# The projection of p moved from the keys stage into the last block of each tile, and the output formed and stored in halves

## The reference

```
h = h + (sum_b sigmoid(gate_b) * (branch_b @ W_b)) @ W_out
h = h + PEER(RMSNorm(h))                               # sum over 128 experts per token of w * v_row
h = h + sigmoid(RMSNorm(h) @ W_g) * (p[i] @ W_p)       # p: (1024, 256), W_p: (256, 1024)
```

## Time and profile before

| what | us |
|---|---|
| median of three runs | 3938.55 |
| the profiled execution's own time | 3932.46 |
| its span | 3930.7 |
| keys stage | 0 to 239 |
| branches stage | 240 to about 765 |
| late stage, before rows are fetched | to about 976 |
| rows being fetched and used | to 3898 |
| last block of tile 7 | 3898 to 3930.7 |

### The profile page before, as it was taken

The page is one execution under the profiler, slowest core; times in us unless marked ns, Lnnn a source line. Parts: engine busy times, 40 slices in busy tenths (PEclk is TensorE's granted clock), DMA queues, the critical chain, the costliest instruction groups (busy, mean ns, idle before and its releaser), DMA issues. The chain is left out here.

```text
span 3930.7 us, 31118 instructions
## 1 busy us (share of the span) xinstructions
PE 3095.3 (79%) x7816; PEld 1408.4 (36%) x7816; DVE 2684.5 (68%) x5254; ACT 1381.2 (35%) x3577; POOL 1214.4 (31%) x1092
## 2 busy tenths in 40 slices
PE   8979999898789988966888878888766656566556
PEld 4545555543334334422333333333322222222222
DVE  3335555312577777776888787877688888888984
ACT  3223333201344433444443342433444334334332
POOL 0000000000333324443443343444244444443442
PEclk9988998799899999988999888899888789878887
DMA  4330101145999999999999999999999999999995
GB/s 160 120 143 27 41 27 45 64 182 197 381 405 413 409 368 413 409 424 426 414 426 426 426 410 405 419 425 426 367 401 412 427 426 412 427 426 395 426 427 247
DMA packets 213925, 1299.35 MB, mean 331 GB/s; under 512 B 24720, under 2 KB 38288, under 8 KB 69520
## 3 DMA queue, kind: packets, MB, share of 16 engines
q0 software_dynamic: 147456, 1073.81, 65.7%
q1 hardware_dynamic: 60560, 211.34, 14.1%
q10 hardware_dynamic: 5760, 12.59, 0.8%
HBM read 1257.80 MB, written 39.85 MB: 330 GB/s over the span
## 5 line engine op out<-in xcount | busy, mean ns | idle before, releaser
L1311 PE MATMUL l_acc<-l_rows,l_diag 128*128 128x512 f32 x2560 | 1414.0, 695 | 704.9 <-ACT l_diag L1445 696.9
L1213 POOL DMA_INDIRECT l_rows<-in_peer_uv,l_at x1024 | 1197.0, 1169 | 1686.0 <-DVE l_acc L1591 1038.0
L1581 DVE SCALAR_TENSOR_TENSOR l_rows<-l_rows,l_xn 128x1024 f32<-128x1024 f32 x1024 | 1220.3, 1223 | 201.9 <-DMA l_rows<-in_peer_uv,l_at 143.6
L1311 PEld LDWEIGHTS l_acc<-l_rows,l_diag 128*128 128x128 f32 x2560 | 526.2, 217 | 1532.7 <-ACT l_diag L1445 999.0
L1591 DVE SCALAR_TENSOR_TENSOR l_acc<-l_rows,l_wts,l_acc 128x1024 f32<-128x1024 f32 x384 | 493.5, 1285 | 204.8 <-ACT l_wts L1441 204.8
L1437 ACT ACTIVATE l_dots<-l_dots 128x2 f32<-128x2 f32 x512 | 103.6, 202 | 1032.5 <-DVE l_rows L1581 1029.6
L1206 POOL CAST l_at<-l_expert 128x16 uint32<-128x16 f32 x64 | 17.3, 270 | 976.6 <-DVE l_expert L1567 976.4
L117 PE MATMUL l_pa<-all_ring,l_xt 128*128 128x512 f32 x656 | 294.4, 600 | 8.4 <-DMA l_xt<-kept_xnt 8.4
L1441 ACT ACTIVATE l_wts<-l_dots,l_gates 128x1 f32<-128x1 f32 x1024 | 293.5, 287 | 16.8
L117 PE MATMUL l_pa<-l_ring,l_xt 128*128 128x512 f32 x624 | 280.6, 601 | 20.4 <-DMA l_xt<-kept_xnt 13.6
L1445 ACT ACTIVATE l_diag<-all_ident,l_wts 128x128 f32<-128x128 f32 x640 | 257.0, 402 | 21.0
(11 more groups left out here) (243 smaller groups left out, 2824.8 us busy)
## 6 DMA issues: line engine op xcount, KB each, us to landing
l_ring<-in_w_late SPq DMA_DIRECT2D x48, 1024.0 KB, 9.4
all_ring<-in_w_late SPq DMA_DIRECT2D x48, 1024.0 KB, 8.9
l_rows<-in_peer_uv,l_at POOLq DMA_INDIRECT x1024, 16.7
l_yt<-kept_yt SPq DMA_DIRECT2D x48, 256.0 KB, 7.7
kept_s<-l_yt ACTq DMA_DIRECT2D x32, 256.0 KB, 7.5
l_s_in<-kept_s SPq DMA_DIRECT2D x64, 128.0 KB, 6.9
mix_w_branches<-in_w_branches_kept SPq DMA_DIRECT2D x8, 768.0 KB, 4.6
kept_yt<-b_yt SPq DMA_DIRECT2D x8, 768.0 KB, 3.7
```

Source lines behind the costliest of these rows:

```text
L1213: pool.indirect_dma_start(out=rows[:, r % SLOTS, :], out_offset=None, in_=A["peer_uv"], in_offset=bass.IndirectOffsetOnAxis(ap=at[:, c % 2 ...
L1311: ins = pe.matmul(acc2[:, hs], diag[n_pe(r) % DIAGS][:], rows[:, r % SLOTS, D + half * HB:D + (half + 1) * HB], start=first, stop=last)
L1581: dve.scalar_tensor_tensor(out=u, in0=u, scalar=1.0, in1=xn[:, t % 2, :], op0=ALU.mult, op1=ALU.mult, accum_out=dots[:, n:n + 1]).then_inc ...
```

## The change

The keys stage loses the projection: its loads of p and W_p, the four products, ScalarE's copy, the store. The DRAM array kept_pp is gone. In the late stage a job pproj for each half stands in slot s+2, between hturn and pgate, and writes to a PSUM tile of pb. W_p is loaded into sgk after the last score job of group 1 and again after that of group 2; the p of each tile is loaded three slots before hturn. VectorE multiplies the sigmoid with the PSUM tile and adds it to acc in halves, two slots after each pgate, and SP stores each half. The sigmoid of group 2's first gate also waits for the last pproj of tile 1, and group 2's jobs begin two slots later (136 in place of 134).

```diff
@@ keys_stage, TensorE
-                pe.wait_ge(pt_in, t * 16 + 16)
-                pe.wait_ge(wp_in, 16)
-                for half in range(2):
-                    hs = slice(half * HB, (half + 1) * HB)
-                    last = matmuls(pe, p_xt[:, hs], [(pt[:, n, :], wp[:, n, hs]) for n in range(2)])
-                last.then_inc(Z["pp_done"], 1)
@@ keys_stage, ScalarE
-                act.wait_ge(Z["pp_done"], t + 1 + FIRST)
-                act.wait_ge(pp_out, t * 16 + FIRST)
-                to(act.copy(pp[:], p_xt[:]), "pp_ready")
@@ keys_stage, SP
-                sp.wait_ge(Z["pp_ready"], t + 1 + FIRST)
-                sp.dma_start(X["pp"][t], pp[:]).then_inc(pp_out, 16)
-                if more:
-                    sp.dma_start(pt[:], A["p_t"][t + 1]).then_inc(pt_in, 16)
@@ Plan
-            begin = self.first + len(PLE_TILES[0]) * NSEL // 2 + 6
+            begin = self.first + len(PLE_TILES[0]) * NSEL // 2 + 8
             self.add((t,), "hturn", 1.8, pb=2, t=t)
             for half in range(2):
+                self.add((t, half), "pproj", 1.8, pb=1, t=t, half=half)
+            for half in range(2):
                 self.add((t, half), "pgate", 6.9, pa=1, chunk=c + 2 * half, n_chunks=2, t=t, half=half)
...
             self.of["hturn", t].slot = slot + 1
             for half in range(2):
+                self.of["pproj", t, half].slot = slot + 2
                 self.of["pgate", t, half].slot = slot + 3 + half
@@ late_stage, SP
+            def load_wp(n):
+                score = plan.of["score", n + 1, 4 * len(GROUPS[n + 1]) - 1]
+                sp.wait_ge(pb_done, score.pb[0] + 1)
+                sp.dma_start(wp, A["ple_proj"]).then_inc(wp_in, 16)
+            def load_p(t):
+                if t > 1:
+                    sp.wait_ge(pb_done, plan.of["pproj", t - 2, 1].pb[0] + 1)
+                sp.dma_start(p_t[:, t % 2, :, :], A["p_t"][t]).then_inc(pt_in[t % 2], 16)
...
+                    if s == plan.of["hturn", t].slot - 3:
+                        load_p(t)
+                    for half in range(2):
+                        if s == plan.of["pgate", t, half].slot + 2:
+                            store_half(t, half)
+                for n in range(len(PLE_TILES)):
+                    if s == plan.of["score", n + 1, 4 * len(GROUPS[n + 1]) - 1].slot + 1:
+                        load_wp(n)
@@ late_stage, TensorE
+            def project(job):
+                n = [n for n, tiles in enumerate(PLE_TILES) if job.t in tiles][0]
+                pe.wait_ge(wp_in, (n + 1) * 16)
+                pe.wait_ge(pt_in[job.t % 2], (job.t // 2 + 1) * 16)
+                hs = slice(job.half * HB, (job.half + 1) * HB)
+                matmuls(pe, into_pb(job.pb[0])[:], [(p_t[:, job.t % 2, k, :], wp[:, k, hs]) for k in range(2)]).then_inc(pb_done, 1)
@@ late_stage, VectorE
-            def output(t):
-                for half in range(2):
-                    freed_pa(dve, plan.of["pgate", t, half].pa[0])
-                dve.wait_ge(pp_in, (t + 1) * 16)
-                order(tt(o[:], o[:], ht[:], ALU.mult))
-                tt(acc[:, t % ACCS, :], acc[:, t % ACCS, :], o[:], ALU.add).then_inc(out_ready, 1)
+            def output(t, half):
+                hs, n = slice(half * HB, (half + 1) * HB), plan.of["pproj", t, half].pb[0]
+                freed_pa(dve, plan.of["pgate", t, half].pa[0])
+                dve.wait_ge(pb_done, n + 1)
+                evacuate(n, tt(o[:, hs], o[:, hs], pb[n % 4][:], ALU.mult))
+                tt(acc[:, t % ACCS, hs], acc[:, t % ACCS, hs], o[:, hs], ALU.add).then_inc(out_ready, 1)
```

More of the change, by code:

```diff
@@ L215, in keys_stage @@
         p_k, p_v, p_a, p_kt, p_f, p_b = (pb(f"p_{n}", [P, HB]) for n in ("k", "v", "a", "kt", "f", "b"))
[L216 to L218 removed]
+        wk_in, wv_in, wa_in, gain_in, x_in, tab_in = (sem(n) for n in ("wk_in", "wv_in", "wa_in", "gain_in", "x_in", "tab_in"))
+        next_w_in, xnt_out, v_out, kt_out = (sem(n) for n in ("next_w_in", "xnt_out", "v_out", "kt_out"))
+        Z = {n: sem(n) for n in ("rms_ready square_ready xs_ready xt_done xnt_ready k_done v_done a_done v_ready va_ready k_ready kt_done "
                                  "kt_ready kf_ready kb_ready f_done b_done b_saved f_state ksq_ready kss_ready krms_ready ka_ready kat_done kat_ready "
@@ L263, in _ @@
             sp.wait_ge(next_w_in, 16 * T)
-            for s in (pp_out, xnt_out, v_out, kt_out):
+            for s in (xnt_out, v_out, kt_out):
                 sp.wait_ge(s, 16 * T + FIRST)
@@ L1043, in late_stage @@
         row_in = [sem(f"row{n}_in") for n in range(SLOTS)]
-        pp_in, out_done = sem("pp_in"), sem("out_done")
+        wp_in, pt_in, out_done = sem("wp_in"), [sem(f"pt{n}_in") for n in range(2)], sem("out_done")
         pa_done, pb_done = sem("pa_done"), sem("pb_done")
@@ L1143, in load_h, with store_half @@
                 sp.wait_ge(h_out[i], nth(g, i) * 16)
-                wait(sp, out_done, (t - ACCS + 1) * 16)
+                wait(sp, out_done, (t - ACCS + 1) * 32)
                 sp.dma_start(acc[:, t % ACCS, :], X["h"][t]).then_inc(acc_in[t % ACCS], 16)
[L1147 to L1154, removed]
+            def load_wp(n):
[6 more added lines that the diff above has]
+                sp.dma_start(p_t[:, t % 2, :, :], A["p_t"][t]).then_inc(pt_in[t % 2], 16)
+            def store_half(t, half):
+                hs = slice(half * HB, (half + 1) * HB)
+                sp.wait_ge(out_ready, 2 * t + half + 1)
+                sp.dma_start(A["out"][t][:, hs], acc[:, t % ACCS, hs]).then_inc(out_done, 16)
             load_group(0)
@@ L1192, in _ @@
                 for t in range(T):
-                    if s == plan.of["pgate", t, 1].slot:
-                        load_pp(t)
-                    if s == plan.of["pgate", t, 1].slot + 3:
-                        store_tile(t)
-            sp.wait_ge(out_done, T * 16)
+                    if s == plan.of["hturn", t].slot - 3:
[6 more added lines that the diff above has]
+                        load_wp(n)
+            sp.wait_ge(out_done, T * 32)
         @block.gpsimd
@@ L1316, in _ @@
             programs = {"gate": gate, "proj": proj, "turn": turn, "out": out, "xt": turn_normed, "query": query, "qturn": turn_query, "score": score,
-                        "hturn": turn_sum, "pgate": gate_product}
+                        "hturn": turn_sum, "pproj": project, "pgate": gate_product}
             for s in range(plan.n_slots):
@@ L1332, in sigmoid_gate @@
                 act.wait_ge(pa_done, job.pa[0] + 1)
+                if job.g == 2 and job.n == 0:
+                    act.wait_ge(pb_done, plan.of["pproj", PLE_TILES[0][-1], 1].pb[0] + 1)
                 if job.n:
@@ L1387, in norm_sum @@
                 act.wait_ge(h2_ready, t + 1)
-                wait(act, out_ready, t)
                 wait(act, prms_ready, t)
@@ L1409, in sigmoid_sum @@
                 act.wait_ge(pa_done, n + 1)
-                wait(act, out_ready, job.t)
+                wait(act, out_ready, 2 * (job.t - 1) + job.half + 1)
                 act.activation(o[:, job.half * HB:(job.half + 1) * HB], pa[n % 2][:], ACT.Sigmoid, scale=prms[:, 2:3]).then_inc(pa_free[n % 2], 1)
@@ L1526, in reciprocal_rms @@
                 dve.wait_ge(prstd_ready, job.t + 1)
-            def output(t):
-                for half in range(2):
-                    freed_pa(dve, plan.of["pgate", t, half].pa[0])
-                dve.wait_ge(pp_in, (t + 1) * 16)
-                order(tt(o[:], o[:], ht[:], ALU.mult))
-                tt(acc[:, t % ACCS, :], acc[:, t % ACCS, :], o[:], ALU.add).then_inc(out_ready, 1)
-                dve.wait_ge(out_ready, t + 1)
+            def output(t, half):
[4 more added lines that the diff above has]
+                tt(acc[:, t % ACCS, hs], acc[:, t % ACCS, hs], o[:, hs], ALU.add).then_inc(out_ready, 1)
+                dve.wait_ge(out_ready, 2 * t + half + 1)
             def top16(scores, values, where):
@@ L1623, in _ @@
                 for t in range(T):
-                    if s == plan.of["pgate", t, 1].slot + 2:
-                        output(t)
+                    for half in range(2):
+                        if s == plan.of["pgate", t, half].slot + 2:
+                            output(t, half)
                 for q, part in plan.parts[s]:
```

11 lines of the change are left out of this document (5 added, 6 removed).

## The result

| | median us | runs | range |
|---|---|---|---|
| before | 3940.34 | 4 | 3936.40 to 3942.30 |
| after | 3918.01 | 4 | 3916.56 to 3920.55 |

The ratio is 0.9945, 95% interval 0.9928 to 0.9962: 22 us faster, where 3941 (3925 to 3957) was forecast. The profiled execution of the changed kernel took 3920.55 us.

The account below looks back on a forecast made before the run. The late stage was taken as bound by DMA bytes, the keys stage and the end as chains. Terms -5.7 + 17 - 1.5 + 0 - 1.2 - 6 = +2.6 us gave a median of 3941 us, range 3925 to 3957.

Parts of the forecast that it names:

- Keys stage: Keys stage: shorter chain and last tile save 12.5 us, clock falling in all seven transitions gives back 6.8; net -5.7 us.
- the forecast's best end of -12.5: Keys stage: the end of its range where the clock stays as now, falling in three of seven transitions; -12.5 us.
- Tiles 2 to 6: Late stage: -1.5 us at tile 2, 0 for other tiles under full transfers, -1.2 for bytes; together -2.7.
- Tile 0: Late stage, first tile: TensorE waits for the late W_p load, transfers run empty 9 + 8 us; +17 (0 to +30).
- The equal share: Tile 0: reading that gives SP's queue 212 GB/s, W_p landing at 1705, a term of about 3 us; weighed, not adopted.
- Rival A: Tile 0: the wait for W_p is covered, costing 0 to 3 us; sum about -13, 3926 us, faster; chance 0.26.
- Rival B: Tile 0: TensorE's whole 29 us shift reaches the end; sum +15, 3953 us, slower; chance 0.28 with the clock case.
- Tile 2's wait: Tile 2: W_p takes 9.4 us, sum and pgate come 2 to 3 us late; +2.5, with -4 for kept_pp's load: -1.5.
- Tail: After the last row: warmer pgate -2 us, shorter work and half-size store after it -4; together -6 (-8 to -3).
- Base: Whole kernel: sum made against the profiled 3932.46 us, then added to the median 3938.55, 6.1 us above it.

Follow-up runs that it names:

- before_again: The kernel before, unedited, timed and profiled a second time: 3937.07 us, ratio 0.9998; its profiled execution took 3942.48 us.
- wp_both: wp_first with the projection of tiles 0 and 2 two slots later, between the two gate products: 3896.15 us, ratio 0.9900 against the kernel before.
- after_again: The changed kernel, unedited, timed and profiled a second time: 3918.03 us, ratio 0.9959 against the kernel before.
- begin_134: wp_both with group 2's jobs beginning at slot 134 again in place of 136: 3897.20 us, ratio 0.9903 against the kernel before.
- no_load: The kernel before without the late stage's load of kept_pp and VectorE's wait for it (output lacks the projection): 3924.00 us, ratio 0.9975.
- wp_first: The changed kernel with W_p for tiles 0 and 1 issued right after the wait for group 1's last score: 3899.47 us, ratio 0.9911 against the kernel before.

## Why the prediction was wrong

**Keys stage, the failed step.** "I take it that the clock then falls in all seven: 4 more at 1.70 us, 6.8 us given back." The chain was right: the warm period went from 25.97 to 24.65 us, 1.32 per tile where 1.30 was worked out, and with the last tile's 3.4 that is the -12.5. The clock fell in three transitions, as often as in the profile before, and cost 0.28 us each. So the clock's part gained 5.1 - 0.8 = 4.3 us where it was to lose 6.8, and the stage went below the forecast's best end of -12.5; these two parts make 16.8 of the 17.6 us by which the stage ended earlier. I had counted how long TensorE is lightly loaded, and not asked which work the low stretch falls on; the chain of VectorE beside it was in the earlier trace rows. The profile before had the fewest slow k products of the seven such traces, by luck; against before_again, with five, the gain is larger still: -22.2 at row 0. The rule of the Trainium skill ("TensorE: Matmul & The Clock Gate", the section on HAM oscillation), that gaps between bursts bring the lower clock back, is what led me to all seven. Three of seven fell here, and the price was set by the work that the lower clock fell on.

**Tiles 2 to 6, the second failed step.** It stood in three terms (-1.5 at tile 2, 0 for the others, -1.2 for bytes, together -2.7) and measured -14.3 and -17.8. "The windows around them are full of transfers, so I count 0": this was read off windows of 300 us. In windows of 20 us the transfers run dry behind the gates: 9.8 us of 60 at tiles 2 and 3 before, 3.4 after; 1.4 us of 20 at tile 4 (2960 to 2980) and 1.6 at tile 6 (3612 to 3632) before, none and 0.4 after. By the experiments: the wait for kept_pp 3 to 6 us, 0.8 MB less about 2 us (an estimate at 420 GB/s), TensorE kept at work ahead of the gate about 5 us, the halves at most 3. Together they come to 13 to 16 of the 14 to 18 us, each from single profiled executions, so the shares are rough. The third stood in the sum with the wrong sign: pproj was "0, at the worst +5", a load on TensorE; in the tail the same effect had been priced (-2) and was found.

**Tile 0, right, a little small.** Forecast: issue behind the branch tiles, idle TensorE of about 25 us, 9 + 8 us of empty transfers, +17. Measured: 28.86 us idle, 18.2 us of empty windows, +17.7 and +20.1 us from row 192 to 320, 21.9 us by wp_both's median. W_p took 26.4 us where about 24.5 was worked out. The equal share that the prediction weighed for SP's queue is not what the trace shows, and the packets show why. Queues of the changed kernel from 1677 to 1704 (packets, MB, share), the row fetches (q0) and SP's loads (q1):

```profile
q0 software_dynamic: 1007, 7.28, 63.8%
q1 hardware_dynamic: 1161, 3.15, 29.2%
```

The two queues moved nearly as many packets, but those of SP's loads hold 2.7 KB on average and those of the rows 7.2 KB. Rival A, the covered wait, is refuted by the 18.6 us that the earlier load was worth. Rival B, the whole shift of 29 us reaching the end, is refuted too, but less widely than its number says: beyond 7 to 8.5 us of cover each us did reach the end.

**Tile 2's wait, right**: W_p took 9.4 us and TensorE waited 5.20 us for it. From hturn to the first gate product it is 17.55 us where it was 14.75, so 2.8 us late where 2 to 3 were forecast; the cost is not visible beside the gain. **Tail, right**: from hturn to the end 31.0 us before and 24.0 after, -6.9 against -6. Row 1023 to the end shows -4.7 since the last sums of the profiled execution took 5.97 us in place of 3.70; after_again, where they take 3.70, shows -7.1 against the first profile of the kernel before and -8.7 against before_again. **Base**: the median's 6 us above the profiled execution were noted and treated as an offset. By before_again they were in part slow k products, which the change could make cheap, and in part a slower row stage; that rests on two profiled executions.

**Left open.** Rows 384 to 544, after tile 1's block, take 460.9 to 464.6 us in the seven traces with the new late stage and group 2 at slot 136, and 458.3 to 461.0 in the six with the old one: a loss of some 3 us on average, smaller than the 4 to 6 us that begin_134's expectation gives. begin_134's trace (459.1 us) shows no such loss, but its median does not tell it from wp_both. And the split of no_load's 10 us is by differences of one profiled execution each. Why the low stretch of the keys stage begins in the k product with the projection and ahead of it without is seen in every trace, and no run here explains it.

## What to carry to other kernels

Moving products out of a chain-bound stage is worth the chain's own shortening plus whatever the clock's low stretch was costing; ask which instruction that stretch lands on, not how often it comes. Where the bytes seem to bound a stage, read windows of 20 us around each block that holds up the engines, and treat work that fills TensorE's pause ahead of a long product as a possible gain. A load whose buffer comes free late is issued ahead of the other waits of the engine that issues it, or its consumer moves behind independent work: here that was worth another 22 us (3896.15 us).

## What the runs showed of the hardware that was not expected

- Useless products paid: 3.6 us of TensorE's time in each of six tiles, 8 us off the kernel (3930.78 to 3922.89); 6 of them are placed in the two traces.
- A low stretch of the clock in the keys stage cost 1.70 us when it met the k product and 0.28 us when it met the small products ahead of it.
- Beside the row fetches a load of 1 MB took 26.4 us, with 1.57 MB ahead of it in the same queue (2.62 MB in 26.4 us, about 100 GB/s of 425). Issued ahead of those 1.57 MB it still took 27.0 us in wp_first, behind as many bytes of an earlier load. At tile 2, with nothing ahead of it, it took 9.4 us.
- The two queues then moved nearly as many packets (1161 and 1007), but 3.15 and 7.28 MB.
- Two profiled executions of one kernel differ by 10.1 us (the kernel before) and 4.3 us (the changed one); with the projection in the keys stage the number of slow k products is three, four or five of seven.
